# Strassen's seven products for three eighths of the inner dimension of six gate and up tiles

## The reference

```python
def swiglu(h, w_gate, w_up, w_down):
    return (jax.nn.silu(h @ w_gate) * (h @ w_up)) @ w_down

x = x + swiglu(rms_norm(x, norm_ffn[i]), ffn_w_gate[i], ffn_w_up[i], ffn_w_down[i])
```

## Time and profile before

| | |
|---|---|
| median of 3 runs | 1201.69 us (1201.59 to 1203.84) |
| profiled execution | 1201.46 us, span 1199.7 us |
| TensorE busy | 1194.4 us, 5350 matmuls |
| VectorE busy | 855.3 us |
| ScalarE busy | 583.4 us |
| GpSimd busy | 54.5 us |
| HBM read and written | 232.02 MB, 7.34 MB |

### The profile page before, as it was taken

How to read it: one execution, slowest core, us unless ns; L and a number is a source line. 1 busy time by engine, 2 the same in 40 slices (tenths; PEclk the granted TensorE clock), 3 DMA queues, 4 the chain that set the end, 5 groups by cost and what they waited for, 6 DMA issues and landing times.

```text
span 1199.7 us, 14649 instructions
## 1 busy us (share of the span) xinstructions
PE 1194.4 (100%) x5350; PEld 989.6 (82%) x5350; DVE 855.3 (71%) x1113; ACT 583.4 (49%) x719; POOL 54.5 (5%) x101
## 2 busy tenths in 40 slices
PE   9999999999999999999999999999999999999998
PEld 7878888888888888888888888888888888888887
DVE  5898989899757587686577677667656565656654
ACT  7556475665545644444444444444344444444442
POOL 1302021020000200000000000000000000000000
PEclk9999999999999999999999999999999999999999
DMA  8667576675769766666666676666565656565673
GB/s 281 194 200 210 175 225 194 200 228 177 224 192 284 245 194 183 204 193 187 194 199 186 189 205 194 181 204 196 177 209 180 208 178 208 180 206 176 189 248 108
DMA packets 136298, 240.08 MB, mean 200 GB/s; under 512 B 17026, under 2 KB 24756, under 8 KB 136244
## 3 DMA queue, kind: packets, MB, share of 16 engines
q1 hardware_dynamic: 136212, 239.39, 64.9%
q10 hardware_dynamic: 32, 0.01, 0.0%
HBM read 232.02 MB, written 7.34 MB: 200 GB/s over the span
## 4 chain that ended last, share of the span: by engine, by line
PE 99%; DVE 1%; ACT 0%; issue 0%; DVEq 0%; ACTq 0%
PE acc L1236 94%; PE R L1236 1%; PE Z L1236 1%; PE T L1282 1%; PE acc L1264 1%; DVE w_lo L805 0%; PE T L1302 0%; DVE squares L868 0%; PE acc L1346 0%; PE T L1275 0%; PE Z L1282 0%; PE acc L1418 0%; PE acc L1426 0%; PE Z L1292 0%; PE T L1292 0%; ACT w_hi L542 0%
## 5 line engine op out<-in xcount | busy, mean ns | idle before, releaser
L542 ACT ACTIVATE w_hi<-raw 128x1024 fp32r<-128x1024 f32 x425 | 448.9, 1059 | 534.8 <-PE acc L1236 514.9
L805 DVE TENSOR_TENSOR w_lo<-raw,w_hi 128x1024 fp32r<-128x1024 f32 x425 | 517.1, 1224 | 262.7 <-ACT w_hi L542 260.0
L1236 PE MATMUL acc<-w_hi,xT_hi 128*128 128x512 f32 x1200 | 470.1, 392 | 0.7 <-DVE w_lo L805 0.6
L1236 PE MATMUL acc<-w_hi,xT_lo 128*128 128x512 f32 x1200 | 467.2, 389 | 0.0
L1236 PE MATMUL acc<-w_lo,xT_hi 128*128 128x512 f32 x1200 | 467.0, 389 | 0.0
L1236 PEld LDWEIGHTS acc<-w_hi,xT_hi 128*128 128x128 f32 x1200 | 225.3, 188 | 48.3 <-DVE w_lo L805 2.4
L1236 PEld LDWEIGHTS acc<-w_hi,xT_lo 128*128 128x128 f32 x1200 | 225.2, 188 | 47.6
L1236 PEld LDWEIGHTS acc<-w_lo,xT_hi 128*128 128x128 f32 x1200 | 225.4, 188 | 45.7
L1236 PE MATMUL acc<-w_hi,hT_hi 128*128 128x512 f32 x352 | 136.9, 389 | 0.0
L1236 PE MATMUL acc<-w_lo,hT_hi 128*128 128x512 f32 x352 | 136.9, 389 | 0.0
L1236 PE MATMUL acc<-w_hi,hT_lo 128*128 128x512 f32 x352 | 136.9, 389 | 0.0
(11 more groups left out here) (177 smaller groups left out, 664.3 us busy)
## 6 DMA issues: line engine op xcount, KB each, us to landing
raw<-in_sb_w_in SPq DMA_DIRECT2D x93, 512.0 KB, 4.4
raw<-in_ffn_w_gate SPq DMA_DIRECT2D x88, 512.0 KB, 3.7
raw<-in_ffn_w_up SPq DMA_DIRECT2D x88, 512.0 KB, 3.8
raw<-in_ffn_w_down SPq DMA_DIRECT2D x88, 512.0 KB, 4.1
raw<-in_sb_w_out SPq DMA_DIRECT2D x32, 512.0 KB, 4.7
raw<-in_ple_w_gate SPq DMA_DIRECT2D x32, 512.0 KB, 4.2
w_scratch<-w_blocks SPq DMA_DIRECT2D x16, 192.0 KB, 5.1
w_side<-w_scratch SPq DMA_DIRECT2D x64, 48.0 KB, 2.0
```

What stands on the lines that cost most here:

```text
L542: act.activation(w_parts[0][:, slot(u), 0:n, :], raw[:, slot(u), 0:n, :], ACT.Copy).then_inc(hi_ready, 1)
L805: dve.tensor_tensor(w_parts[1][:, slot(u), 0:n, :], raw[:, slot(u), 0:n, :], w_parts[0][:, slot(u), 0:n, :].bitcast(F32), ALU.subtract).th ...
L1236: last = pe.matmul(acc[pair][tb][:, :], parts[a][:, c, tb * P:(tb + 1) * P], w_parts[w][:, slot(u), i, :], start=(start and i == 0 and n = ...
```

## The change

Of the 11 tiles of gate and up, tiles 2 to 7 are computed in three pairs. A pair has two matrices, gate and up, each of 2048 rows by 1024 columns, so six matrices (`MATRICES`) follow one another between tile 1 and tile 8. A matrix is 16 blocks of rows; block c is taken with block c + 8 in one step, eight steps (`KINDS` = "SNSNNSNN").

An N step does what was done: two units, each one block by 1024 columns, 12 matmuls each, but for the banks. An S step is one of Strassen's scheme in Winograd's form: with the two token blocks as rows and blocks c, c + 8 as the inner halves, and the two tiles as columns, 7 products instead of 8. It takes four units: two differences T1, T3 of weight blocks (`T13`), the two plain blocks, two more differences T2, T4 (`T24`), and one plain block, with 2, 2, 2 and 1 products of 3 matmuls. GpSimd makes the differences. Both kinds add into eight banks, P1 to P8, all of PSUM; after a matrix VectorE adds them up to the four results (`combine`), in part before its end and in part while the next matrix runs. The sums of token blocks (S1 to S4) are made once, in tile 1 (`tokens`).

The raw blocks of an S step stand in one buffer, `raw[:, 0:2]`; the raw blocks of N steps in four places (`n_raw`). All tiles of the feed-forward part are transposed through HBM now: two transposes of 128x512 (`block_hidden`), store, fetch, copy and difference. `hT` is split in two parts so that buffers of the pairs lie where its second part stands later. The loops of TensorE and SP are unrolled.

The core of the diff:

```diff
+    PAIRS, KH = 3, KD // 2
+    KINDS = "SNSNNSNN"
+    SM, NM = KINDS.count("S"), KINDS.count("N")
+    AT = [4 * KINDS[:i].count("S") + 2 * KINDS[:i].count("N") for i in range(KH + 1)]
+    S_AT, N_AT = [a for a, kind in zip(AT, KINDS) if kind == "S"], [a for a, kind in zip(AT, KINDS) if kind == "N"]
+    MU = AT[KH]
+    MATRICES = 2 * PAIRS
...
+            T13, T24 = row("T13", [P, 2, NT], F32, pairs), row("T24", [P, 2, NT], F32, pairs)
+            raw_n = row("raw_n", [P, 2, 2, NT], F32, pairs)
+            spare = row("spare", [P, 4, NT], F32, pairs)
+            stage2, part_a, part_b = spare[:, 0:2, :], spare[:, 2, :], spare[:, 3, :]
...
+        n_raw = [raw[:, 2, :, :], raw[:, 3, :, :], raw_n[:, 0, :, :], raw_n[:, 1, :, :]]
...
+            def store_hidden(j):
+
+                sp.wait_ge(h_blocks_ready, TB * (j + 1))
...
+            def fetch_hidden(j):
+
+                sp.wait_ge(h_stored, 16 * (j + 1))
...
+            def load_s(s):
+
+                sp.wait_ge(lo_ready, s_unit(s - 1, 3) + 1 if s > 0 else C2 - 2)
+                for i in range(2):
+                    sp.dma_start(raw[:, i, :, :], pair_columns(s // SM, s % SM + KH * i)).then_inc(s_landed, 16)
...
+                        sp.wait_ge(lo_ready, n_unit(n - 2, i) + 1)
+                    sp.dma_start(n_raw[m % 4], pair_columns(n // NM, SM + n % NM + KH * i)).then_inc(n_landed[m % 4], 16)
...
+            for n in range(NQ):
+                matrix, k = divmod(n, NM)
+                tile = matrix if matrix > 0 else 1
+                s = matrix * SM + sum(a < N_AT[k] for a in S_AT) - 1
+                if N_AT[k] - 4 in S_AT and s + 1 < SQ:
+                    load_s(s + 1)
+                if n + 2 < NQ:
+                    load_n(n + 2)
+                if matrix % 2 == 0:
+                    if k == 1:
+                        store_hidden(tile)
+                    if k == 2:
+                        fetch_hidden(tile)
+                    if matrix > 0 and k == 3:
+                        store_hidden(tile + 1)
+                    if matrix > 0 and k == 4:
+                        fetch_hidden(tile + 1)
...
+            def differences(s):
+
+                a, b = 0, 1
+                pool.wait_ge(s_landed, 32 * (s + 1))
+                if s == 0:
+                    pool.wait_ge(tokens_ready, 1)
+                else:
+                    pool.wait_ge(lo_ready, s_unit(s - 1, 0) + 1)
+                pool.tensor_tensor(T13[:, 0, :], raw[:, a, 1, :], raw[:, a, 0, :], ALU.subtract).then_inc(differences_ready, 1)
+                pool.tensor_tensor(T13[:, 1, :], raw[:, b, 1, :], raw[:, a, 1, :], ALU.subtract).then_inc(differences_ready, 1)
+                if s > 0:
+                    pool.wait_ge(lo_ready, s_unit(s - 1, 2) + 1)
+                pool.wait_ge(differences_ready, 4 * s + 1)
+                pool.tensor_tensor(T24[:, 0, :], raw[:, b, 1, :], T13[:, 0, :], ALU.subtract).then_inc(differences_ready, 1)
+                pool.wait_ge(differences_ready, 4 * s + 3)
+                pool.tensor_tensor(T24[:, 1, :], raw[:, b, 0, :], T24[:, 0, :], ALU.subtract).then_inc(differences_ready, 1)
...
+                act.wait_ge(unit_used, U - RING + 1)
+                if KINDS[k] == "S":
+                    s = matrix * SM + S_AT.index(AT[k])
+                    if i == 0 or i == 2:
+                        act.wait_ge(differences_ready, 4 * s + 2 + i)
+                    else:
+                        act.wait_ge(s_landed, 32 * (s + 1))
+                    source = (T13[:, :, :], raw[:, 0:2, 0, :], T24[:, :, :], raw[:, 1:2, 1, :])[i]
+                    n = 1 if i == 3 else 2
...
+                    if matrix % 2 == 0 and v == 14:
+                        hidden_hi(matrix if matrix > 0 else 1)
+                    if matrix % 2 == 1 and matrix > 1 and v == 4:
+                        hidden_hi(matrix)
...
+                    dve.transpose(h_blocks[:, tb, :, :].rearrange("p b (c i) -> p b c i", i=Q),
+                                  source[:, tb, :].rearrange("p (c b j) -> p b c j", b=QN, j=Q)).then_inc(h_blocks_ready, 1)
...
+            def combine(matrix, v):
+
+                U0 = C2 + matrix * MU
+                up = matrix % 2 == 1
+                now = 4 * (matrix // 2)
+
+                def add(to, a, bank, signal):
+                    dve.tensor_tensor(to, a, banks[bank], ALU.add).then_inc(signal, 1)
+
+                first = S_AT[-1] + 7
+                if v == first:
+                    dve.wait_ge(product_read[P1], matrix + 1)
+                    dve.wait_ge(unit_used, U0 + S_AT[-1] + 3)
+                    add(part_a, part_1, P6, product_read[P6])
+                if v == first + 1:
+                    dve.wait_ge(product_read[P6], matrix + 1)
+                    add(part_b, part_a, P7, product_read[P7])
+                if v == first + 2:
+                    dve.wait_ge(product_read[P7], matrix + 1)
+                    add(junk[:, :] if up else stage2[:, 1, :], part_b, P5, product_read[P5])
+                    add(part_a, part_a, P5, product_read[P5])
+                if v == MU + 2:
+                    dve.wait_ge(unit_used, U0 + MU)
+                    add(part_1 if up else stage[:, 0, :], part_1, P2, product_read[P2])
+                    add(part_b if up else stage[:, 1, :], part_b, P4, product_read[P4])
+                if v == MU + 3:
+                    dve.wait_ge(product_read[P5], 2 * matrix + 2)
+                    add(part_a if up else stage2[:, 0, :], part_a, P3, product_read[P3])
+                    to = junk[:, :] if up else stage2[:, 1, :]
+                    add(to, to, P8, product_read[P8])
+                if up and v in (MU + 4, MU + 5):
+                    dve.wait_ge(pair_gated, now + 4)
+                    for i in (2 * (v - MU) - 8, 2 * (v - MU) - 7):
+                        dve.wait_ge(product_read[(P2, P4, P3, P8)[i]], matrix + 1)
+                        part = (stage, stage2)[i // 2][:, i % 2, :]
+                        dve.tensor_tensor(part, part, (part_1, part_b, part_a, junk[:, :])[i],
+                                          ALU.mult).then_inc(pair_multiplied, 1)
...
+            def pair_matrix(matrix):
+
+                for v in range(MU):
+                    pair_lo(matrix, v)
+                    combine(matrix, v)
+                    if matrix > 0:
+                        combine(matrix - 1, MU + v)
+                    if matrix == 0 and v == 2:
+                        times_up(1, C2 - 1)
+                        p_lo()
+                    if matrix % 2 == 0:
+                        tile = matrix if matrix > 0 else 1
+                        if v == 7:
+                            block_hidden(tile)
+                        if v == 14:
+                            hidden_lo(tile)
+                        if matrix > 0 and v == 15:
+                            block_hidden(tile + 1)
+                    else:
+                        if matrix > 1 and v == 5:
+                            hidden_lo(matrix)
+                        if v - 1 in SIG_AT:
+                            pair_gate(matrix, SIG_AT.index(v - 1))
+
...
+                    if j == AFTER_PAIRS and k == 0:
+                        for bank in ((P2, P4), (P3, P8))[part]:
+                            pe.wait_ge(product_read[bank], MATRICES)
...
+            def bank_left(matrix, bank):
+
+                if matrix > 0:
+                    pe.wait_ge(product_read[bank], matrix * (2 if bank == P5 else 1))
...
+            def seven_products(matrix, k):
+
+                low = [a[:, k, :] for a in xT]
+                high = [a[:, k + KH, :] for a in xT]
+                a11, a12, a22 = [a[:, 0:P] for a in low], [a[:, 0:P] for a in high], [a[:, P:2 * P] for a in high]
+                s1, s2, s3, s4 = [[a[:, n, k, :] for a in S] for n in range(4)]
+                for i, factors in enumerate((((P5, s1), (P7, s3)), ((P1, a11), (P2, a12)), ((P6, s2), (P4, a22)), ((P3, s4),))):
+                    U = s_unit(matrix * SM + k, i)
+                    pe.wait_ge(lo_ready, U + 1)
+                    for n, (bank, factor) in enumerate(factors):
+                        if k == 0:
+                            bank_left(matrix, bank)
+                        last = three_terms(bank, factor, U, n, k == 0, k == SM - 1 and bank in (P1, P5, P6, P7))
+                    last.then_inc(unit_used, 1)
+
```

349 lines of the change are left out of this document (294 added, 55 removed).

## The result

The changed kernel takes 1253.19 us (median of 4, 1252.02 to 1255.54) beside 1202.72 us of the kernel before (1201.59 to 1203.84): a ratio of 1.0425, 95% interval 1.0409 to 1.0441. The forecast was 1217 us with a range of 1193 to 1236. The direction was right, the loss more than three times what I had forecast. The profiled execution took 1252.02 us (span 1250.3).

The account below looks back on a forecast made before the run. The prediction took gapless TensorE as the bound, 0.2267 us a matmul. Removed matmuls -12.2, S steps +18.0, tile through HBM +8.5 and exit +1.3 gave +15.6 on 1201.46 us: 1217 us, range 1193 to 1236.

Parts of the forecast that it names:

- the exit: Leaving the pairs, once: the first plain unit waits for P2 and P4 to be read, 1.3 us.
- the entry: Start of the pairs after tile 1: claimed to cost nothing, since the banks are free or read in time.
- v6: Unit 6 of a matrix's 22, counted from 0, where the second S step starts: TensorE forecast to wait 1.9 us.
- v15: Unit 15, in the third S step; in matrices 0, 2, 4 its low part was forecast 2.1 us late behind the tile.
- GpSimd's lone difference: One 128x512 subtraction on GpSimd meeting nothing on VectorE: taken as 1.15 us.
- (a): Second S step of each matrix, its raw blocks having one buffer: 3.0 us late, six times, 18.0 us.
- T13's chain: Low part, reload, two GpSimd differences, copy, low part before the second S step: 1.9 us late in each matrix.
- half held: GpSimd's fourth difference, for T24, held by VectorE in half the cases: 1.1 us a matrix.
- the rival with 0.12: VectorE and GpSimd block each other at their shared port, 48.0 us a matrix instead of 41.5: 1230 or 1238; chance 0.12.
- (b): Tile stored to HBM and fetched back in matrices 0, 2 and 4, landing late for the third S step: 8.5 us.
- The clock rival: TensorE's clock falls in nine stalls, each bringing one unit at 1.2 GHz, 24 us more: 1241; chance 0.05.
- VectorE's load: VectorE's summed work in a matrix: 34.2 of 41.5 us, so the engine fits and only the order decides.

Follow-up runs that it names:

- e5_order_late: e1_tile_late with each matrix's steps in the order S N N S N S N N: 1232.45 us, against 1232.85 for e1_tile_late.
- e1_tile_late: Changed kernel with the copy and low part of the tile fetched through HBM at unit 19 instead of 14 in even matrices: 1232.85 us.
- h3_three_gpsimd: h1_three_vector with the 72 differences on GpSimd again: 1219.09 us.
- h1_three_vector: Changed kernel with differences on VectorE, single-factor unit ahead of T24, raw halves reloaded early, tile at unit 19, P3 summed earlier; still three S steps: 1203.49 us.
- h2_two_tile10: h1_three_vector's arrangement with two S steps a matrix, but the tile picked up at unit 10: 1212.8 us, against 1197.64 with it at unit 19.
- e2_narrow: Changed kernel with GpSimd's 72 differences computed on 32 of 512 columns, the rest left zero, all waits and loads kept: 1225.84 us.
- g1_two: Changed kernel with two S steps a matrix, single-factor unit ahead of T24, raw halves reloaded early, tile at unit 19, differences still on GpSimd: 1207.15 us.

## Why the prediction was wrong

**Right.** The removed matmuls (54, 12.2 us), the exit (1.3 forecast, 1.4 measured), no cost at the entry, the places of the long waits (v6, v15, the exit), and that the sum comes out slower. GpSimd's lone difference (1.25 us against 1.15) and the load (5.05 against 5.4) were close.

**(a) The S steps: 18.0 us forecast, 36.2 measured.** T13, with v0 to v6: 11.4 forecast (6 x 1.9), 18.4 measured. T24, with v6 to v14: 6.6 forecast (6 x 1.1), 17.8 measured, of which 5.6 belong to the sigmoids below. T13's chain, step by step, in matrix 2: v3's low part done at 3.4 us after the end of the matrix before (1.9 forecast); reload 5.05 us (5.4); two differences 3.2 us (2.45), the first of them held; TensorE starts v6 at 14.1 (12.1). The step that failed is "VectorE has done v2 and then stands at the additions of P2 and P4": the chain began on an engine with nothing behind. VectorE entered the matrix late, since T24 of the matrix's first S step had kept it (ScalarE had waited 1.55 us for it, and the low part of v1 took 1.72), and the sums for P5 stood ahead as well; it began v2's low part at 0.4. Matrix 0 shows the same step alone: its two differences weren't held (1.28 and 1.27 us), but two sums and the low part of another tensor stood ahead on VectorE, v3's low part was done 3.9 us after v0's start, and TensorE started v6 at 14.1. And the sum had no term for VectorE held by GpSimd, which the next two paragraphs tell. I had worked out one step from a rested start and multiplied it by six.

**T24: half held was wrong, it is always held.** I took the fourth difference as held in half the cases, 1.1 us. It was held in 18 of 18, by one low part each time, since it starts when VectorE takes up the low part of the unit that T13 has just made ready: an order that the kernel imposes itself, not a chance. Nor was it held over two or three low parts, as one row of before had suggested: in this kernel the two engines took turns, one instruction each. That is no rule, as e5_order_late shows (4.37 us over three VectorE instructions).

**The port: the rival with 0.12 had half of the mechanism.** "That VectorE waits for GpSimd no row shows" was true of before, and I let it keep the chance low. The changed kernel's rows show it: 2.30 us for a low part of 1.22. The Trainium skill's page "SBUF — State Buffer", section "Who interferes with whom", says just this (a VectorE instruction with two SBUF inputs contends with a GpSimd one that reads SBUF; the pair of ports is an exclusive lock, and the order of issue decides who blocks), and on this the trace agrees in both directions. The rival's criterion, that each also blocks the other, was met. That its sum comes near (1230 without the tile's wait, 1232.9 in e1_tile_late) doesn't show that the port was the bound: VectorE was busy for 70% of the stretch, and it stood for some 17 us, 2.9 a matrix, where the rival had 6.5 by putting all of its work with two SBUF inputs and all of GpSimd's one behind the other. The rest fits the chain, in which GpSimd's own 1.25 to 2.23 us lie on TensorE's way; but in e1_tile_late one of the two engines or the other was at work for 95% of the first five matrices, and no run parts a chain from a pair of engines that is nearly full. What the runs part: by h3_three_gpsimd against h1_three_vector GpSimd's differences cost 15.6 us more than the same work on VectorE.

**(b) The tile: 8.5 us forecast, 20 measured** (e1_tile_late). In matrix 2 the store left 1.1 us after the end of v9 (0.7 forecast), and the fetch started 8.3 us after it. The step that failed is "At the lighter share of 0.65 I take 4.4": 0.65 is the mean share of the stage, but between store and fetch it was 0.99, since the S reload and the N loads go out with it; and the other end of my range, the 7.0 us of the earlier trace rows, would still have been too short. From the fetch's start to the copy it took 4.7 us (5.75 forecast), and from there to v15 3.5, as forecast. h2_two_tile10 shows that even 4.1 us don't save the place one unit behind the fetch.

**What was left out:** 5.2 us in v14 to v0 (e1_tile_late), nearly all of it TensorE's five waits at v0 for P5's bank, 4.5 us with the longest 1.1; and the sigmoids' circle over one buffer, by which the odd matrices are 1.8 us longer than the even ones from v6 to v14 (5.6 us, within the 17.8). The prediction had these operations in VectorE's sum, not in its order. What opens the circle again isn't shown: h1_three_vector has the sigmoids at the same units and not this difference, while e2_narrow, in which no low part is held, still has it; the order of the units differs between them, and other things too.

**The clock rival** (0.05, 1241) had its mechanism and no price: 17 us of clock, at most some 1.3 us of time.

**VectorE's load.** The forecast's 34.2 of 41.5 us "fits" gave each engine's sum and asked only for single late places. The sum itself wasn't wrong: h1_three_vector, 8 us of differences fuller in each matrix and without a single instruction held by GpSimd, loses 11.8 us and not 61. What failed was the order.

Still open: how e2_narrow's gain divides between GpSimd's own time and VectorE's standing, and what the odd matrices of h1_three_vector wait for at v9 and v10.

## What to carry to other kernels

An idle engine isn't free help when it and the busy one hold each other off: GpSimd's differences of 1.25 us took 0.8 us each from VectorE in g1_two, more than the 0.68 us that VectorE needs for one, and where they took less, in the changed kernel (0.25), TensorE waited for them. Before giving work away, price it also as standing time of the engine that it is to relieve. And work a periodic schedule through two periods, with the second starting from what the first left behind; a place that needs a store to land and be fetched wants several units of distance, not one, and here it cost nothing to give them.

Saving less can win: two Strassen steps in eight with their distances kept are 0.4% faster than before, three were 0.14% slower than it in the best kernel tried (h1_three_vector, 1.0004 to 1.0024).

## What the runs showed of the hardware

- A GpSimd subtraction of 128x512 fp32 takes 1.25 us alone and 2.23 us (2224 to 2252 ns, 18 of 18) when it starts just after a VectorE difference with two SBUF inputs; the VectorE difference behind it takes 2.30 instead of 1.22 us. VectorE's sums from PSUM kept their 0.68 us beside GpSimd's differences.
- In the changed kernel the two engines took turns, one instruction each (no difference over 2.28 us, no low part over 2.32). In e5_order_late GpSimd was held over three VectorE instructions in a row twice (4.37 and 4.41 us).
- In the changed kernel's pairs the granted clock stood at 0.50 seven times, for 3.4 us (four times) or 6.8 us (three times): around the end of each of the six gaps of TensorE from 2.6 us up (from 2.4 us before it to 1.4 us behind it), and behind one gap of 1.8 us, but not at the two of 2.0 us. Where the next operands are late as well this costs little: 17.1 us of lost clock, 1.3 us of time, within the spread of the runs.
- A 512 KB store to HBM and its fetch: 4.07 us from one to the other at a DMA share of 0.90 and 297 GB/s in between (h2_two_tile10), 8.30 us at 0.99 and 353 GB/s (changed kernel).
